# Rotary halves by ScalarE, two norm sums by VectorE, and products of constants at the joins of a two-block transformer kernel

## What is computed

```python
def rope(x, pos):                       # head dimension 64, half = 32
    x1, x2 = xf[..., :half], xf[..., half:]
    return jnp.concatenate([x1 * cos - x2 * sin, x2 * cos + x1 * sin], axis=-1)

mem_n = rmsnorm(mem, mem_norm_g)
for layer in range(2):
    u = rmsnorm(h, norm_g[layer, 0])
    mem_kv = mem_n @ w_mem_kv[layer]
    y = mixer_window_attn(...) if layer == 0 else mixer_hgrn2(...)
    h = h + rmsnorm(y, norm_g[layer, 1])
    f = conv_ffn(rmsnorm(h, norm_g[layer, 2]), ...)
    h = h + rmsnorm(f, norm_g[layer, 3])
```

## Time and profile before

| | |
|---|---|
| median of 3 runs | 2539.05 us (2537.50 to 2540.21) |
| profiled execution | 2541.4 us, span 2539.6 us |
| granted TensorE clock, mean | 0.981 of 2.4 GHz |
| TensorE busy | 2445.4 us, 96% |
| GpSimd busy | 1461.2 us, 58% |
| VectorE busy | 1205.0 us, 47% |
| ScalarE busy | 621.9 us, 24% |
| read from HBM | 210.51 MB, 84 GB/s |

### The profile page before, as it was taken

One profiled execution on the slowest core, in us unless ns is written; L12 is line 12 of the kernel. 1 busy time (PEld: TensorE's weight loads), 2 busy tenths in 40 slices (PEclk: granted clock), 3 DMA queues, 4 the chain that ended last, 5 costly groups with the idle time before them and its releaser, 6 DMA issues.

```text
span 2539.6 us, 33035 instructions
## 1 busy us (share of the span) xinstructions
PE 2445.4 (96%) x12352; PEld 2007.8 (79%) x12352; DVE 1205.0 (47%) x1993; ACT 621.9 (24%) x1266; POOL 1461.2 (58%) x1475
## 2 busy tenths in 40 slices
PE   8999999999999999899999999999999988999997
PEld 6877778887888887687778888877888876888886
DVE  3335654334203224576367551055777872765502
ACT  3233321002102110355121110034666532211000
POOL 7654546666666665453558776631323534787761
PEclk9999999999999999999999999999999988999998
DMA  4222222232222322121223232212112111222321
GB/s 162 85 98 88 80 83 95 96 100 92 92 99 93 123 93 82 51 76 59 71 79 100 92 99 98 94 50 67 59 58 67 59 50 59 91 94 98 100 91 58
DMA packets 59762, 214.64 MB, mean 85 GB/s; under 512 B 6624, under 2 KB 6752, under 8 KB 59488
## 3 DMA queue, kind: packets, MB, share of 16 engines
q1 hardware_dynamic: 56880, 206.68, 24.5%
q10 hardware_dynamic: 2736, 5.96, 0.7%
HBM read 210.51 MB, written 2.10 MB: 84 GB/s over the span
## 4 chain that ended last, share of the span: by engine, by line
PE 91%; DVE 6%; ACT 2%; issue 1%; DMA 0%; POOL 0%; DVEq 0%; ACTq 0%; POOLq 0%
PE acc L552 24%; PE acc L554 24%; PE acc L553 24%; PE ps_s L703 2%; PE ps_o L731 2%; PE ps_t L717 2%; PE ps_s L995 1%; PE acc L770 1%; PE acc L772 1%; PE acc L771 1%; PE ps_o L1056 1%; PE ps_t L651 1%; PE ps_s L981 0%; PE ps_s L770 0%; PE ps_s L772 0%
## 5 line engine op out<-in xcount | busy, mean ns | idle before, releaser
L509 POOL CAST w_hi<-w_raw 128x512 fp32r<-128x512 f32 x702 | 451.7, 672 | 826.4 <-DMA w_raw<-stream 826.3
L552 PE MATMUL acc<-h_hi,w_hi 128*128 128x512 f32 (+1 forms) x1860 | 734.7, 395 | 3.6 <-DVE h_lo L1473 1.2
L554 PE MATMUL acc<-h_hi,w_lo 128*128 128x512 f32 (+1 forms) x1860 | 712.9, 383 | 0.0
L553 PE MATMUL acc<-h_lo,w_hi 128*128 128x512 f32 (+1 forms) x1860 | 711.8, 383 | 0.0
L511 POOL TENSOR_TENSOR w_lo<-w_raw,w_hi 128x512 fp32r<-128x512 f32 x384 | 509.1, 1326 | 205.2 <-ACT w_hi L1415 205.2
L513 POOL TENSOR_TENSOR w_lo<-w_raw,w_hi 128x512 fp32r<-128x512 f32 x384 | 530.6, 1382 | 0.0
L552 PEld LDWEIGHTS acc<-h_hi,w_hi 128*128 128x128 f32 x1860 | 351.1, 189 | 74.2 <-issue 4.6
L554 PEld LDWEIGHTS acc<-h_hi,w_lo 128*128 128x128 f32 x1860 | 350.1, 188 | 70.9
L553 PEld LDWEIGHTS acc<-h_lo,w_hi 128*128 128x128 f32 x1860 | 351.1, 189 | 68.1 <-issue 3.6
L1547 DVE COPY y_all<-acc 128x512 f32<-128x512 f32 x32 | 22.1, 692 | 279.4 <-PE acc L554 248.2
L552 PE MATMUL acc<-hid_hi,w_hi 128*128 128x512 f32 x352 | 138.9, 395 | 0.0
(11 more groups left out here) (334 smaller groups left out, 3646.0 us busy)
## 6 DMA issues: line engine op xcount, KB each, us to landing
w_raw<-stream SPq DMA_DIRECT2D x384, 512.0 KB, 3.3
toeplitz<-ext_in ACTq DMA_DIRECT2D x16, 256.0 KB, 3.7
out<-x_res SPq DMA_DIRECT2D x4, 512.0 KB, 2.6
x_res<-x_in SPq DMA_DIRECT2D x3, 512.0 KB, 6.8
mem<-mem_in ACTq DMA_DIRECT2D x1, 1024.0 KB, 6.8
consts<-consts_in SPq DMA_DIRECT2D x1, 784.0 KB, 9.4
x_res<-x_in SPq DMA_DIRECT2D x2, 256.0 KB, 5.0
rope<-rope_in ACTq DMA_DIRECT2D x1, 512.0 KB, 7.7
```

The source lines that it names most:

```text
L509: nc.gpsimd.tensor_copy(hi[:, half], raw[:, half]).then_inc(hi_made, 1)
L552: nc.tensor.matmul(ps, hi, x_hi[:, k, 0:cols], start=(k == 0), stop=False)
L553: nc.tensor.matmul(ps, hi, x_lo[:, k, 0:cols], start=False, stop=False)
L554: mm = nc.tensor.matmul(ps, lo, x_hi[:, k, 0:cols], start=False, stop=(k == st.kt - 1))
```

## The change

- ScalarE writes the swapped halves of each rotary tile, in four copies of 32 partitions from one group of partitions to another, two of them with the scale -1. Two buffers (`normed`) take turns. The `rot` products go. VectorE multiplies in place by the sine. The plan starts at block 1 instead of 4.
- For the memory ScalarE makes the high halves and squares in place, VectorE the low halves and seven additions; one ones-product stays. For b_in the norm uses the same form as ffn_in.
- In the joins before ffn_in0, b_in and ffn_in1, `turning` issues products of two constant matrices, 128 x 128, into a free bank: four, two and nine.
- Work behind the attentions is cut anew (`xq_cut`, `B_IN_CUT`), and pieces also stand behind the first two groups of scores. b_in's blocks 4 and 5 use two of the extra banks and come ahead of its attention; b_out's block 4 uses one too.
- In the first recurrence head four tiles move behind the first scores. In the last head the sum of head 6 comes before two lead steps, and ScalarE's `head_rest` behind the root. Four output tiles are split between other steps. Eleven tiles of b_out's block 4 come before its last lead step, and two slots are counted out together (`done`).

```diff
-WIDE = {"ffn_in0", "ffn_in1"}
-EXTRA = 3
+WIDE = {"ffn_in0": (4, 5, 6), "ffn_in1": (4, 5, 6), "b_in": (6, 5), "b_out": (4,)}
...
-        B_IN_TILES = 3
+        B_IN_CUT = [19, 21, 23, *range(25, 5 * DT + 1)]
...
-            def rotate(st, i):
-
-                take_t(rope_done, i + 1)
-
-                pe.wait_ge(st.free, i + 1)
-                src = q_win[:, i, :] if i < DT else k_win[:, i - DT, :]
-                nc.tensor.matmul(ps_t[:], const("rot"), src, start=True, stop=True).then_inc(rope_rot, 1)
...
                 for j in range(begun, LOOK):
                     scores(units, j)
+                    for work in also.get(j - LOOK, []):
+                        work()
...
+            def turning(st, count):
+
+                bank_free(st, 0)
+                for _ in range(count):
+                    nc.tensor.matmul(banks[st.banks[0]][:, 0:P], const("ones"), const("ident"), start=True, stop=True)
+
...
                 block_tiles(st, tiles - 3, tiles, x_hi, x_lo)
+                if then is not None:
+                    turning(then, 4)
                 pe.wait_ge(y_sq, DT * n["y"])
                 square_sums(sq[:, (DT - 1) % 2, :], True).then_inc(y_sum, 1)
 
+                if then is not None:
+                    turning(then, 2)
                 out_free()
...
                 mm.then_inc(y_rstd, 1)
+                if then is not None:
+                    turning(then, 9)
...
             def mem_sums():
-                for i in range(DT):
-                    sum_square(i, DT, const("ones"), MEM, mem)
+                summed_norm(MEM)
...
-            lead(st, h_hi, h_lo, waits_for(h_ready, n["h"]), input_norm, halves=4)
+            lead(st, h_hi, h_lo, waits_for(h_ready, n["h"]), halves=5)
...
-            block_tiles(st, first, first + B_IN_TILES, h_hi, h_lo)
-            pe.wait_ge(st.free, X_HEADS)
+            block_at(st, X_HEADS, h_hi, h_lo)
+            summed_norm()
+            block_at(st, X_HEADS + 1, h_hi, h_lo)
+            block_tiles(st, first + 2 * DT, first + B_IN_CUT[0], h_hi, h_lo)
+            pe.wait_ge(st.free, X_HEADS + 2)
...
+                if h == HG_HEADS - 1:
+                    head_sum(h - 1)
                 head_in(h + 1, 2)
-                if h:
+                if 0 < h < HG_HEADS - 1:
                     head_sum(h - 1)
-                else:
+                if h == 0:
 
                     head_in(1, 3)
-                    head_in(1, 4)
                 head_scores(h, 0)
                 head_keys(h, 0)
                 if h:
                     head_in(h + 1, 3)
+                else:
+                    head_in(1, 4)
...
+            st = stages["b_out"]
+            lead_tiles, early = BANKS * st.kt, st.kt - 1
             out_lead(10)
             head_out(HG_HEADS - 1)
+            block_tiles(st, lead_tiles, lead_tiles + 4, o_hi3, o_lo2)
             head_sum(HG_HEADS - 1)
-            out_lead(11)
-            mixer_out(stages["b_out"], o_hi3)
+            block_tiles(st, lead_tiles + 4, lead_tiles + early, o_hi3, o_lo2, done=0)
+            out_lead(11, done=1 + early // SLOT_TILES)
+            block_tiles(st, lead_tiles + early, lead_tiles + st.kt, o_hi3, o_lo2)
+            mixer_out(st, o_hi3, stages["ffn_in1"], BANKS + 1)
...
+            quarter, st = HEAD_DIM // 2, stages["a_in"]
+            for i in range(10):
+                src = q_win[:, i, :] if i < DT else k_win[:, i - DT, :]
+                act.wait_ge(st.free, i + 1)
+                if i >= 2:
+                    act.wait_ge(rope_ready, i - 1)
+                for a in range(0, P, quarter):
+                    b = a + quarter if a % HEAD_DIM == 0 else a - quarter
+                    nc.scalar.activation(normed[a:a + quarter, i % 2, :], src[b:b + quarter, :], ACT.Copy,
+                                         scale=-1.0 if b > a else 1.0).then_inc(rope_half, 1)
...
+            def mem_total():
+
+                for i in range(1, DT):
+                    dve.wait_ge(x_sq, n["x"] + i + 1)
+                    step.wait()
+                    step(nc.vector.tensor_tensor(rstd_in[:, 0:MEM], mem[:, 0, :] if i == 1 else rstd_in[:, 0:MEM], mem[:, i, :], ALU.add),
+                         x_total if i == DT - 1 else None)
...
-                    for i in range(X_HEADS):
-                        split_out(i, o_hi3, x_o)
+                    split_out(0, o_hi3, x_o)
                 head_in(h + 1, 4)
+                if h == HG_HEADS - 2:
+                    split_out(1, o_hi3, x_o)
                 head_scores(h, 2)
+                if h == HG_HEADS - 2:
+                    split_out(2, o_hi3, x_o)
+                    split_out(3, o_hi3, x_o)
```

More of the change, by code:

```diff
@@ L125, in place_accumulators @@
         for c in range(st.cbs):
-            extra = name in WIDE and BANKS <= c < BANKS + EXTRA
-            bank = c if extra else turn % BANKS
+            extra = BANKS <= c < BANKS + len(WIDE.get(name, ()))
+            bank = WIDE[name][c - BANKS] if extra else turn % BANKS
             turn += not extra
@@ L564, in bank_free @@
                     pe.wait_ge(stages["v1"].free, c + 1)
-                elif c == BANKS:
+                elif c == BANKS and st.name != "b_out":
                     pe.wait_ge(s_used, n["unit"])
@@ L615, in lead, with block_tiles @@
                         then(k)
-            def block_tiles(st, first, end, x_hi, x_lo, cols=T):
+            def block_tiles(st, first, end, x_hi, x_lo, cols=T, done=1):
                 for tile in range(first, end):
@@ L865, in conv_mlp @@
                 st = stages[f"ffn_in{layer}"]
[L866 removed]
+                lead(st, h_hi, h_lo, waits_for(h_ready, n["h"]), halves=4 + 2 * layer)
                 block_at(st, BANKS, h_hi, h_lo)
@@ L879, in conv_mlp, with mixer_out @@
                         block_at(st, c, hid_hi, hid_lo)
-                last_block(st, hid_hi, hid_lo, ffn_tmp)
-            def mixer_out(st, x_hi):
-                for c in range(BANKS, st.cbs - 1):
+                last_block(st, hid_hi, hid_lo, ffn_tmp, None if layer else stages["b_in"])
+            def mixer_out(st, x_hi, then, first=BANKS):
+                for c in range(first, st.cbs - 1):
                     block_at(st, c, x_hi, o_lo2)
-                last_block(st, x_hi, o_lo2, square)
+                last_block(st, x_hi, o_lo2, square, then)
             st = stages["a_in"]
@@ L1330, in _, with mem_halves @@
             x_root()
+            quarter, st = HEAD_DIM // 2, stages["a_in"]
[8 more added lines that the diff above has]
+                                         scale=-1.0 if b > a else 1.0).then_inc(rope_half, 1)
+            def mem_halves(tiles):
+                act.wait_ge(st.free, st.cbs)
+                act.wait_ge(mem_loaded, 16)
+                for i in tiles:
+                    nc.scalar.activation(h_hi[:, i, 0:MEM], mem[:, i, :], ACT.Copy, scale=param("mem_g", i)).then_inc(x_hi_made, 1)
             def mem_squares(tiles):
@@ L1335, in mem_squares, with mem_part @@
                     act.wait_ge(h_ready, 3 * DT + i + 1)
-                    squared(mem[:, i, :], MEM, mem)
-            also = {MEM_INPUT + 1 + i // 2: lambda i=i: mem_squares([i, i + 1]) for i in range(0, DT, 2)}
-            also[MEM_SUMS] = lambda: root(n["sq"], 1.0 / D, small["eps_d"][:], MEM)
+                    nc.scalar.activation(mem[:, i, :], mem[:, i, :], ACT.Square).then_inc(x_sq, 1)
+                    n["x"] += 1
+            def mem_part(i):
+                if i < DT:
+                    mem_halves([i, i + 1])
+                if i:
+                    mem_squares([i - 2, i - 1])
+            also = {MEM_INPUT + i // 2: lambda i=i: mem_part(i) for i in range(0, DT + 1, 2)}
+            also[MEM_SUMS] = lambda: root(n["x"] // DT, 1.0 / D, small["eps_d"][:], MEM, summed=x_summed)
             attention(units_win + units_x[0], probs2, probs2_t, also)
@@ L1956, in _ @@
                 step(nc.vector.memset(t_[:], 0.0))
-            attention(units_x[1], probs2, {b_in_turn(j): [lambda j=j: head_in(0, j)] for j in range(5)})
+            head_in(0, 0)
+            head_in(0, 1)
+            attention(units_x[1], probs2, {min(b_in_turn(j), len(units_x[1]) - 1): [lambda j=j: head_in(0, j)] for j in range(2, 5)})
             dve.wait_ge(pv_done, n["unit"])
```

74 lines of the change are left out of this document (40 added, 34 removed).

## The result

The changed kernel takes 2500.2 us (median of 4 runs, 2496.66 to 2501.05) against 2539.63 before: ratio 0.9842, 95% interval 0.9828 to 0.9857. Timed a second time it took 2497.68 us (median of 4), ratio 0.9846 (0.983 to 0.9862). I had said 2489, range 2475 to 2513: the time lies inside the range, but only four fifths of the 50.3 us that I had added up came.

The account below looks back on a forecast made before the run. TensorE, busy 96% of the span, was taken to bound the kernel, with waits costing twice through a lowered clock. Gains of 11.5 + 6 + 2 + 5.4 + 11.7 + 2.5 + 11.2 = 50.3 us gave 2489 us, range 2475 to 2513.

Parts of the forecast that it names:

- Rotations: In a_in, ten rotation products (8.7 us), their waits (2.4) and a little at either side leave TensorE: gain 11.5 us.
- the upper bound: In a_in, a ScalarE piece of 32 x 512 takes as long as a whole 128 x 512 cast, 0.62 us.
- Start of the window attention: Up to the third group of scores, tiles behind the first two groups gain 6 us; ends 3 and 7.
- Memory norm: Seven ones-products go, TensorE waits 1 us longer for VectorE's seven additions: gain 2 us, ends -3 and 6.
- a rival at 0.08: Memory norm: GpSimd blocks the seven additions, near 1.4 us each, 10 us instead of 4.7; total 2494 us; chance 0.08.
- Joins: Before ffn_in0 and ffn_in1, constant products fit in the waits and the clock holds: gain 2.7 us each, 5.4 together.
- The rival of a clock that falls all the same: At the three joins, constant products at half pace overrun by about 2 us each; total 2506 us; chance 0.14.
- b_in: With its join, up to its attention's end: 19 us to gain, 7.2 given back, taken as 11.7; ends 7 and 15.
- First head: First recurrence head: the 2.8 us wait stays; gain 4.7 us if the clock holds, 0.5 if it falls; 2.5 taken.
- The clock term of 4.7: First recurrence head: four moved tiles keep the array dense around the wait and the clock holds, gaining 4.7 us.
- End of the recurrence: Last heads and lead of b_out: fewer waits, eleven block 4 tiles earlier; gain 11.2 us, ends 6 and 14.
- The wait of about 9: Sign expected in the last head: one TensorE wait of about 9 us where there were several.

Follow-up runs that it names:

- Experiment 5: Changed kernel with the running sum of the memory squares in PSUM, so six of seven additions have one operand there; 2500.07 us.
- experiment 3: Changed kernel without the fifteen products of constants at the three joins; 2506.58 us.
- experiment 6: Changed kernel with the two memsets moved, one ahead of the reciprocal, one inside b_in's attention; 2494.7 us.
- experiment 7: Changed kernel with twelve products of constants in front of the first head's second scores; 2497.15 us.
- experiment 4: Changed kernel with the four tiles of the first recurrence head in front of its first scores again; 2497.9 us.
- experiments 1 to 7: Changed kernel with one edit each, executed once; the first of them put the ten rotations back on TensorE, 2513.59 us.
- experiment 2: Changed kernel with the memory norm's sum as eight products of ones again, no VectorE additions; 2494.77 us.

## Why the prediction was right, and where it was not

**Rotations: right.** 11.5 predicted, 11.5 to 12.1 measured. A piece takes what the whole tile takes, as I had taken it (the upper bound):

```profile
L1351 ACT ACTIVATE normed<-q_win 32x512 f32<-32x512 f32 x32 | 20.2, 630 | 25.0 <-DVE q_win L1611 24.4
```

That is 0.63 us for 32 partitions against 0.62 for 128 in the earlier trace rows; four pieces are 2.5 us a tile. By the Trainium skill, "ScalarE: Activation LUTs", section "What ACT_TABLE_LOAD costs", the engine works at one element per cycle in each lane, so that fewer lanes save nothing: the trace agrees.

VectorE's queue cost 0.4 us in the first trace (a wait for `v_feat` at 1001.09, absent in the second), where I had put 0. I had not asked what the moved work does to VectorE: its thirty rotary products and additions took 22.0 us before and 36.5 in the changed kernel, mostly beside GpSimd's work, for the reason that comes next. In a_in this was nearly free: TensorE waited for VectorE there 0.8 us, as before, and these 0.4.

**Start of the window attention: right,** 6.0 and 6.1 of 6.

**Memory norm: the step that failed is the length of the additions.** I had written "I take the wait as 1 longer" and a gain of 2, from additions at a mean of 0.63 us. They took 0.42 to 1.30, 7.5 us in all where I had 4.7, the wait grew by 3.9 (8.3 instead of 4.38) and the part lost 2.7 and 0.7 in the two traces. The rest of the step holds: with 4.7 in place of 7.5 the wait would have been 5.5 by the same trace, 1.1 longer than before (an estimate). Of the 4.7 us by which the first trace falls short, 2.9 are this wait; the tiles behind it took 2.0 us more than before because of the low clock, where I had 1.3; and 0.9 more was lost at the start of the memory's projection, where TensorE waits 2.1 us for VectorE's low half instead of 1.2, a wait that I had left out.

The mean was of a mixed group. In the trace of before, the sixteen instructions of the earlier trace rows are twelve of 0.42 us with GpSimd idle, three with it busy throughout (1.17 on average) and one of 1.40 with it busy in part. In the changed kernel's trace, the level products of the recurrence (L2106, the same shape, both inputs in SBUF) take 0.42 us where GpSimd is idle all the while (55 instructions) and 1.05 on average where it is busy all the while (6). I had the right mechanism as a rival at 0.08 and 1.4 us an addition, and its 2494 was nearer than my 2489, though as a total by luck: the first head's shortfall helped it there. It came true in kind: four of the seven met a subtraction (1.30), two a cast and one nothing. A price in between was to be had by asking of each row in the group what GpSimd did at that time. That the additions could meet GpSimd was to be seen as well: the earlier trace rows has it busy for 11.6 of that stretch's 23.6 us. The Trainium skill, "SBUF — State Buffer", section "Who interferes with whom", says that a VectorE instruction with two SBUF inputs contends with GpSimd instructions that read SBUF and one with at most one such input, outside the two-port modes, does not, and names casts and tensor-by-scalar operations as ones that can contend as well. Experiment 5 agrees (0.43 with one operand in PSUM, 2.41 instead of 0.62 for the two scalings), and so do the casts of 128 x 512 in the changed kernel's trace (0.43 with GpSimd idle, 0.63 to 0.88 in the six cases with it busy throughout).

**Joins: right and a little large.** 2.2 and 2.1 of 2.7 each. The timeline before ffn_in0, answering to the earlier trace rows:

```profile
1263.30 1.13 PE L861 MATMUL ps_o<-consts,rstd 128*128 128x128 f32 x8
1264.26 2.17 PE L838 MATMUL acc<-consts 128*128 128x128 f32 x18
1266.80 0.47 PE L598 MATMUL acc<-h_hi,w_hi 128*128 128x512 f32 x1 [0.36 <-issue]
```

The broadcasts take 1.13 instead of 2.02, a lead pass 0.47 instead of 0.77, and the second lead step waits 1.1, 0.7 and 1.2 us for the low half, where I had said about 1. The rival of a clock that falls all the same is out, and experiment 3 shows that the constants are the reason.

**b_in: right.** 10.8 of 11.7, with a wait of 3.8 where I had worked out 3.9 and a slow restart behind it. The first trace bears the chain out: 12.35 us from the ones-product to the scores, where I had added up 12.3. I had found that wait and its cause (VectorE's queue with two memsets in it), and did not ask whether it had to be there.

**First head: wrong, and below both of its ends.** "Nothing decides; 2.5" was halfway between 0.5 and 4.7. The wait stayed at 2.8 as said, the clock fell, and the part lost 1.5; in experiment 6, with the same order, it lost nothing. The clock term of 4.7 was well sized (4.0 to 4.9 in experiment 7), but moving tiles ahead of a wait did not keep it up through the wait. The likelier end was the lower one, since nothing runs in the wait. Why the clock fell for longer than before in most traces stays open (experiment 4).

**End of the recurrence: right.** 11.2 predicted; 13.9 and 12.2 in two traces and 11.1 to 11.8 in six experiments. The wait of about 9 came as two, 4.3 and 2.5 in the first trace, 6.6 together in the second and 7.8 to 9.6 in experiments 1 to 7: I had missed that the splits moved to the end of head 6 stand in VectorE's queue ahead of the states of head 6, which its output products wait for.

**Outside every part:** the restart of a_out's lead lost 1.6 in the first trace by the clock alone.

Set out as a sum for the first trace: 50.3 predicted, -4.7 memory norm, -4.0 first head, -1.6 restart, -1.1 joins, -0.9 b_in, +2.7 end of the recurrence, +0.9 elsewhere, makes 41.6. The 2.7 of the recurrence's end is partly luck: the same code gave less in every other trace, 13.7 once and 11.1 to 12.2 otherwise.

## What to carry to other kernels

Work moved from TensorE to VectorE pays its price at the moment at which it runs, not at its mean. Split each group of rows by whether GpSimd was busy, and keep sums that TensorE waits for off VectorE where GpSimd has a block of work (4.6 to 6.6 us here); putting them in PSUM made them short, but brought no gain in time that one run could show. A wait costs less when something runs in it: constant products in a free bank held the clock at three joins (5.6 us) and in the first head (4.0), while real tiles moved ahead of the wait did not. When you find a new wait in a forecast, look at what stands in the late engine's queue: two memsets there were worth 4.2 to 4.9 us.

## What the runs showed of the hardware that was not expected

- One-input operations in SBUF are stretched as well: two scalings of 128 x 256 took 2.41 us beside GpSimd and 0.62 alone. In the changed kernel's trace, products with one PSUM operand (128 x 512, L1609) took 0.69 us in all 120 cases with GpSimd busy throughout and in all 42 with it idle.
- An addition of 128 x 256 with both inputs in SBUF took 1.30 us beside a subtraction of GpSimd (128 x 512), 0.65 beside a cast of it and 0.42 alone.
- With the same code, the same wait of 1.87 us was followed by a fall of the granted clock in the changed kernel's first trace and not in its second, a difference of 1.6 us.
- 1.4 us of waiting ahead of b_in's attention left the clock up, 3.8 us let it fall: the wait's 2.4 us were worth 4.9 in one trace and 4.2 in another. The 1.8 us ahead of the eight memory products of experiment 2 left it up as well.
